# Moving the transposed activations by 64 bytes in SBUF

## The reference

```
# first block
h = rms_norm(x, norm1_g);  u, v, q, k, v2 = split(h @ w_in)
mix = [rms_norm(spatial_gating(gelu(u), gelu(v))), rms_norm(dilated_attention(rope(q), rope(k), v2))]
x = x + mix @ w_out
x = x + peer(rms_norm(x, norm2_g))        # 8 heads, each picks 16 of 128*128 experts per token
    # act = gelu(x . expert_u[e]);  out = sum(g * act * expert_v[e])
x = rms_norm(x, final_norm_g)
# second block, two layers
proj = x @ w_in_2[layer]                   # 4680 columns
oA = stick_breaking_attention(...);  oB = top-64 sparse attention with relative bias(...)
y = [oA * silu(gA), oB * silu(gB)] @ w_out_2[layer]
x = layer_norm(ALPHA * x + y)
```

## Time and profile before

| | |
|---|---|
| median of 3 runs | 1329.18 us (1328.66 to 1329.45) |
| the profiled execution | 1329.18 us, its span 1327.3 us |
| PE busy | 1268.4 us, 96% of the span, 9917 matmuls |
| PEld busy | 1212.0 us, 91% |
| DVE, ACT, POOL busy | 55%, 51%, 50% |
| mean granted TensorE clock | 0.981 |
| read from memory | 215.50 MB, 166 GB/s with what is written |

### The profile page before, as it was taken

The page is one execution under the profiler, slowest core; times in us unless marked ns, Lnnn a source line. Parts: engine busy times, 40 slices in busy tenths (PEclk is TensorE's granted clock), DMA queues, the critical chain, the costliest instruction groups (busy, mean ns, idle before and its releaser), DMA issues.

```text
span 1327.3 us, 26744 instructions
## 1 busy us (share of the span) xinstructions
PE 1268.4 (96%) x9917; PEld 1212.0 (91%) x9917; DVE 727.5 (55%) x1494; ACT 676.5 (51%) x1202; POOL 669.5 (50%) x286
## 2 busy tenths in 40 slices
PE   7988999898999999999999999999999999799996
PEld 5876999898999999999999999999999987699875
DVE  2444149994066666775666656666537632346423
ACT  4555444444566655555554455544544564346552
POOL 6735769999866666663000000000047765567653
PEclk9989999999999999999999999999989999899999
DMA  5724545455544444445666655666564433444432
GB/s 210 259 88 140 193 143 186 162 176 174 193 152 145 142 145 143 144 143 190 191 192 195 195 192 190 192 196 195 178 220 147 140 128 127 156 131 150 142 121 80
DMA packets 59141, 218.59 MB, mean 165 GB/s; under 512 B 6656, under 2 KB 6696, under 8 KB 58688
## 3 DMA queue, kind: packets, MB, share of 16 engines
q1 hardware_dynamic: 56592, 206.07, 47.1%
q0 software_dynamic: 1792, 8.95, 1.8%
q10 hardware_dynamic: 688, 2.62, 0.5%
HBM read 215.50 MB, written 4.21 MB: 166 GB/s over the span
## 4 chain that ended last, share of the span: by engine, by line
PE 82%; issue 7%; POOL 7%; DVE 2%; ACT 2%; DMA 0%; POOLq 0%; DVEq 0%; ACTq 0%
PE A L503 27%; PE W L503 18%; POOL ringl L460 5%; PE A L527 5%; PE A L528 5%; PE A L532 4%; PE W L765 4%; PE A L547 4%; PE A L549 4%; PE A L554 4%; POOL ringl L424 1%; PE W L581 1%; PE W L928 1%; PE W L899 1%; PE W L640 1%
## 5 line engine op out<-in xcount | busy, mean ns | idle before, releaser
L424 POOL TENSOR_TENSOR ringl<-ring,ringh 128x1024 fp32r<-128x1024 f32 x137 | 338.0, 2482 | 183.2 <-ACT ringh L976 176.7
L460 POOL TENSOR_TENSOR ringl<-ring,ringh 128x1024 fp32r<-128x1024 f32 x126 | 321.2, 2555 | 102.6 <-ACT ringh L1136 78.6
L503 PE MATMUL W<-XTh,ringh 128*128 128x256 f32 x1024 | 291.5, 285 | 8.2 <-POOL ringl L460 8.1
L503 PE MATMUL W<-XTl,ringh 128*128 128x256 f32 x1024 | 285.1, 278 | 0.0
L503 PE MATMUL W<-XTh,ringl 128*128 128x256 f32 x1024 | 285.1, 278 | 0.0
L503 PE MATMUL A<-Hh,ringh 128*128 128x256 f32 x1024 | 283.2, 277 | 0.0
L503 PE MATMUL A<-Hl,ringh 128*128 128x256 f32 x1024 | 283.1, 276 | 0.0
L503 PE MATMUL A<-Hh,ringl 128*128 128x256 f32 x1024 | 283.0, 276 | 0.0
L976 ACT ACTIVATE ringh<-ring 128x1024 fp32r<-128x1024 f32 x135 | 142.0, 1057 | 157.3 <-PE A L532 71.2
L503 PEld LDWEIGHTS W<-XTh,ringh 128*128 128x128 f32 x1024 | 194.0, 189 | 10.2 <-issue 9.8
L1136 ACT ACTIVATE ringh<-ring 128x1024 fp32r<-128x1024 f32 x189 | 197.4, 1045 | 0.4 <-DMA ring<-exp_v 0.4
(11 more groups left out here) (263 smaller groups left out, 2108.4 us busy)
## 6 DMA issues: line engine op xcount, KB each, us to landing
ring<-exp_u SPq DMA_DIRECT2D x128, 512.0 KB, 3.2
ring<-exp_v SPq DMA_DIRECT2D x128, 512.0 KB, 3.6
ring<-w SPq DMA_DIRECT2D x72, 512.0 KB, 3.2
ring<-w_out SPq DMA_DIRECT2D x24, 512.0 KB, 3.2
ring<-w_in SPq DMA_DIRECT2D x20, 512.0 KB, 3.4
ring<-w_query SPq DMA_DIRECT2D x16, 512.0 KB, 3.2
skewed<-scratch POOLq DMA_DIRECT2D x1, 2048.0 KB, 11.4
H<-lng POOLq DMA_DIRECT2D x2, 1024.0 KB, 6.7
```

Of the source, the lines that this page charges most:

```text
L424: pool.tensor_tensor(ringl[:, slot, :], ring[:, slot, :], ringh[:, slot, :].bitcast(F32), ALU.subtract)\
L460: pool.tensor_tensor(ringl[:, slot, :], ring[:, slot, :], ringh[:, slot, :].bitcast(F32), ALU.subtract)\
L503: last = pe.matmul(dst, stationary[a], moving[b], start=start and n == 0, stop=stop and n == 2, skip_group_check=True)
```

## The change

The tile XTh, and with it the tiles created between it and the next gap (XTl, gain, RB, GF, bias_s, w_idx2), start at 128 modulo 512 in place of 192. The address of XTh goes from 161472 to 161408, that of XTl from 169664 to 169600. X ends at 161408, so no gap is created there any more. The gap ahead of ring grows from 416 to 480 bytes, so that ring and all tiles behind it keep their addresses. `home` also no longer rounds the base up to a multiple of 32; the three bases that it sees are multiples of 32 before and after. The instructions, their order and their waits are the same on all five queues.

```diff
         def home(first):
-            n = (first - (nc.sbuf_base + 31) // 32 * 32) % 512
+            n = (first - nc.sbuf_base) % 512
             if n:
                 sb(f"gap{nc.sbuf_base}", [P, n // 4])
...
-        home(192)
+        home(128)
         XTh = sb("XTh", [P, KC, T], F32R)
         XTl = sb("XTl", [P, KC, T], F32R)
```

## The result

The changed kernel takes 1343.82 us (median of 4 runs, 1342.05 to 1344.74) against 1328.92 us before (1328.48 to 1329.45): ratio 1.011, 95% interval 1.0097 to 1.0122, so 14.9 us slower. The forecast was 1329.2 us, with 1322 to 1342 as its range. The profiled execution of the changed kernel took 1344.54 us, its span is 1342.7.

What follows compares the result with a forecast made beforehand. TensorE's matmul pace was taken as the bound (busy 96% of the span). Instruction, transfer and wait terms were zero, and the address effect, bounded by -15.6 and +18.5 us, was taken as zero: 1329.2 us, range 1322 to 1342.

Steps and rivals of the forecast that it cites:

- rival B: XTh and XTl matmuls lose their faster pace at 128 bytes; 1341.9 us, up to 1347.7; chance 0.35 whole or part.
- the low pace: Faster of two start-to-start paces of 256-column matmuls in the trace before, 0.1133 us; the down stage has it throughout.
- Its check: Profile after: from 383 us every column at 2.84 us or more, x504 near 59.5 us, down stage keeping 334.8 us.
- I take zero: Central choice for the operand address effect on PE's matmuls: zero, between outer ends of -15.6 and +18.5 us.
- the index products: Last-stage matmuls reading w_idx2 in 64-byte steps: 24 steps at 0.1117 us without a difference, taken as evidence for nothing.
- more to lose than to win: Argument for a slower result: about two thirds of the matmuls already run at the faster pace.
- the high pace: Slower of the two paces of 256-column matmuls, 0.1178 us; all XTh and XTl matmuls at it would add 12.7 us.
- the 512-column matmuls: 912 matmuls with ring moving and XTh or XTl loaded, 0.2292 us each; their bounds were -2.4 to +5.8 us.
- a pace of over 0.118 us: Sign in the profile after that would make the reasoning wrong in size; so would one under 0.1117.
- The stretch x504: Row of 504 matmuls in the up stages, 57.40 us before; near 59.5 us if the slower case held.
- the 2 to 4 us named at most: Give-back from PE's 8.1 us of waits for POOL low parts before 383 us, if PE ran slower.
- 109.2 ns for 256 columns: Skill page's matmul time, columns / 2.4 GHz + 2.5 ns; by it the sum would have room for 24 us less.

Runs made afterwards that it cites:

- the first experiment: All three homes 64 bytes lower than in the kernel before (XTh 128, ring 192, Hh 128), distances unchanged; 1328.77 us against 1328.16, ratio 0.9998.

## Why the prediction was wrong

**What held.** PE's pace as the place of the cost: the other engines kept their busy times, and no wait of PE for another engine grew by more than 0.1 us. That nothing is issued, moved or waited for otherwise. The rounding that goes from `home` moves no address: so the 64 bytes are the whole change. Of rival B, from the two paces of the earlier trace rows, this held: the low pace is lost for XTh and XTl, Hh is untouched. Its check came true, every column at 2.84 us or more and the down stage at 334.8. The experiments show that the distance between the addresses of the moving and the loaded operand sets the pace; that ring's traffic has no part; that the position alone has none. That two read streams meet or miss each other fits this, but no run looks inside.

**The step that failed.** "I take zero, the value of the only rows in which the address varies." Those were the index products, and their moving side is 8 or 16 columns. The prediction said itself that "their pace is that of the load" and then let them decide. They stay flat at 0.1117 us over places at which 256 moving columns differ by 4 to 6%: a pair whose moving side is short does not show what a long one pays, and the question was as open as without them. Against zero stood a positive sign, two steady paces of one instruction in the earlier trace rows, for which I had no explanation other than operands that meet. Given that, the question was whether -64 is a usual distance or a good one. The Hh products were low for 334.77 us without a break, at a distance of -64; "more to lose than to win", as rival B said, was the reading to follow, though those rows did not prove it: the draw could have been luck. In the runs nine of the ten places of the table are slower, eight of them by 3.9% to 5.9% over -64 in the same column of the table, the ninth (+32) by 2.9%.

**Sizes.** Rival B's price was 12.7 us by the high pace, to 18.5 us with the 512-column matmuls. Measured: 14.9 us. By the prediction's own sign, a pace of over 0.118 us, the reasoning was wrong in size too: the high pace was taken as the bound of a loss, and the new paces are others, 0.1200 between the gates and 0.1187 in long rows. The stretch x504, put near 59.5 us, took 60.07.

If all 128 columns went to the 2.88 us of those with gates, that would be 84 x 0.14 + 44 x 0.04 = 13.5 us. In the columns that run ahead the new pace is less (0.1187), and waits for POOL gave 1.6 us back, a little under the 2 to 4 us named at most; 10.0 us are left in the up stages.

The other 5.4 us (2.5 before them, 2.9 after the start of the down stage) are the unit loops and the 512-column matmuls together, less what the clock gave back. After the down stage and ahead of the last 10 us, the granted clock was 0.50, its level of 1.2 GHz, for 27.2 us in the profile of before (966.1 to 969.5, 986.6 to 993.4, 1112.9 to 1116.3, 1140.2 to 1150.4, 1167.5 to 1170.9) and for 20.4 us after (997.4 to 1004.2, 1154.4 to 1164.6, 1181.7 to 1185.1). Half of the difference, up to 3.4 us, is an estimate of what that hid of the cost; such stretches also differ between kernels of equal distances.

In the timeline of the changed kernel's last unit loop, units of 12 such matmuls begin 2.80 us apart, 0.2333 a matmul against 0.2292 in the earlier trace rows:

```profile
1311.41 0.40 PE L527 MATMUL A<-ringh,XTh 128*128 128x512 f32 x1
...
1314.21 0.40 PE L527 MATMUL A<-ringh,XTh 128*128 128x512 f32 x1
```

The rise of 4.1 ns lies inside the bounds of -2.6 and +6.4 that the sum had. There the roles are turned round, and another place is the best of those tried: with XTh at distance 0 two units in a row begin 2.73 us apart in the chain of that kernel, 0.2275 us a matmul, the least that I saw.

```profile
1303.50 0.23 PE A L527
...
1306.23 0.23 PE A L527
```

**The chances.** 0.35 for slower and 0.40 for no change came from giving the same weight to rows that can't show the effect as to rows that show its sign. The range ended at 1342 because the outer end of B was left out with its 512-column part, and that part was real (0.2333 for 0.2292 us). That the measured time lies between B's two ends is partly luck: a pace above B's bound and the time that the clock and POOL gave back worked against each other.

The Trainium skill has TensorE's reads wait for nobody ("SBUF — State Buffer", section "SBUF: two separate sides") and the two operands on independent ports ("TensorE: Matmul & The Clock Gate", section "Step-by-step: what each phase is for"). The runs disagree in effect: the distance of the two operands alone moves the pace from 0.1134 to 0.1201 us. The prediction's estimate from the latter page, 109.2 ns for 256 columns by its section "Wait — 56ns, not 53.3ns?", was reached by no run here.

**What stays open.** Why one distance has two steady paces, and what draws one of them on entering: x504 and columns changed their draw between kernels of equal distances (all low from 391 us in the first experiment, in turns before). Whether a stage at +64 could be kept at the low pace that it showed in a few places is open as well, and so is whether other places have a second pace, since most were run once. What has the period of 256 bytes was not measured either.

## What to carry to other kernels

Where a long row of float32r matmuls bounds a kernel and loads new weights for each, the addresses of the moving and the loaded tile are a tuning knob: read the pace from start to start in the trace, move one tile in small steps through 256 bytes, and pin the good distance, since a tile added between the two shifts it (one added ahead of both moves them together, which cost nothing in the first experiment). Two paces of the same instruction without a wait were the sign here that this is in play. And a row in which the address varies did not speak for a long stream, its own being short: the index products were flat where 256 columns were not.

## What the runs showed of the hardware that was not expected

A matmul of 256 float32r columns that loads a new 128 x 128 float32r operand each time takes 0.1134 us from start to start at the best distance of its two operands, or 0.1178 when the second pace of the same place is drawn, and 0.1178 to 0.1201 us at the other places tried with Hh, 0.1172 to 0.1205 with XTh, at a granted clock of 1.00. The low pace also came up in a few places at -192. The period is 256 bytes. The good place is narrower than 32 bytes to each side (0.1184 at -32, 0.1187 at -96), and 16 bytes off, with starts that are no multiple of 32, it is lost as well (0.1192 at -48, 0.1198 at -80). One of three passes at -128 spoils all three (60.10 us for x504, against 60.07 with all). For 512 columns with the roles turned round the best place tried is distance 0, 0.2275 us against 0.2292 at -64 and 0.2333 at -128.
